# Four edits around the root-mean-square norms of a two-block transformer kernel, and a last residual sum formed by TensorE

## What is computed

```python
def rms_norm(x, g):
    y = x * lax.rsqrt(jnp.mean(x * x, axis=-1, keepdims=True) + 1e-6)
    return y * g

# first block
x = x + gt1 * mix                       # mix = concat(...) @ w_out
x = x + gt2 * swiglu(modulate(x, norm2_g, sh2, sc2), w_ffn_in, w_ffn_out)
# second block
x = x + rms_norm(merged @ w_mix_out, mix_post_g)
h = rms_norm(x, xa_pre_g)
x = x + rms_norm(mem_attention(h, ...), xa_post_g)
h = rms_norm(x, ffn_pre_g)
x = x + rms_norm(conv_ffn(h, ...), ffn_post_g)   # the output
```

## Time and profile before

| | us |
|---|---|
| runs before: lowest, median, highest of 3 | 1684.70, 1688.21, 1689.57 |
| the profiled execution | 1688.94 |
| its span | 1687.3 |

### The profile page before, as it was taken

How to read it: one execution, slowest core, us unless ns; L and a number is a source line. 1 busy time by engine, 2 the same in 40 slices (tenths; PEclk the granted TensorE clock), 3 DMA queues, 4 the chain that set the end, 5 groups by cost and what they waited for, 6 DMA issues and landing times.

```text
span 1687.3 us, 19115 instructions
## 1 busy us (share of the span) xinstructions
PE 1575.8 (93%) x7574; PEld 1243.4 (74%) x7574; DVE 944.2 (56%) x1440; ACT 725.4 (43%) x1124; POOL 139.7 (8%) x98
## 2 busy tenths in 40 slices
PE   8998989798799999999999899999887899999995
PEld 2776767587688888888878677788675688888884
DVE  3665767785744433334555555366656576257744
ACT  4453435675432222223443667455354443234421
POOL 0100212541000000000000011120011000000001
PEclk9999999699999999999999999999998899999997
DMA  9441111101524233222322222233212122332231
GB/s 370 163 162 39 50 38 63 63 1 45 192 100 147 67 111 112 98 75 88 103 100 69 63 72 67 66 122 100 75 42 71 61 90 76 113 107 93 84 103 50
DMA packets 47949, 156.59 MB, mean 93 GB/s; under 512 B 5587, under 2 KB 10323, under 8 KB 47350
## 3 DMA queue, kind: packets, MB, share of 16 engines
q1 hardware_dynamic: 47280, 152.00, 27.1%
q10 hardware_dynamic: 582, 3.38, 0.6%
HBM read 153.26 MB, written 2.10 MB: 92 GB/s over the span
## 4 chain that ended last, share of the span: by engine, by line
PE 74%; DVE 15%; ACT 7%; issue 3%; DMA 1%; POOL 0%; ACTq 0%; DVEq 0%; SPq 0%
PE pall L2079 17%; PE pall L2081 17%; PE pall L2080 17%; PE pall L2115 2%; PE pall L2562 2%; PE pall L2116 2%; PE pall L2117 1%; PE pall L2097 1%; PE pall L2098 1%; PE pall L2099 1%; PE pall L2564 1%; PE pall L2563 1%; DVE wlo L1222 1%; ACT whi L560 1%; DVE R L1235 1%
## 5 line engine op out<-in xcount | busy, mean ns | idle before, releaser
L1222 DVE TENSOR_TENSOR wlo<-raw,whi 128x1024 fp32r<-128x1024 f32 (+2 forms) x261 | 290.2, 1113 | 310.5 <-ACT whi L560 310.4
L560 ACT ACTIVATE whi<-raw 128x1024 fp32r<-128x1024 f32 (+2 forms) x263 | 246.5, 939 | 144.8 <-PE pall L2081 114.4
L2079 PE MATMUL pall<-h5h,whi 128*128 128x512 f32 x320 | 126.1, 394 | 8.4 <-DVE wlo L1222 8.4
L2080 PE MATMUL pall<-h5l,whi 128*128 128x512 f32 x320 | 125.5, 392 | 0.0
L2081 PE MATMUL pall<-h5h,wlo 128*128 128x512 f32 x320 | 125.4, 392 | 0.0
L2079 PE MATMUL pall<-h2h,whi 128*128 128x512 f32 x320 | 124.5, 389 | 0.0
L2080 PE MATMUL pall<-h2l,whi 128*128 128x512 f32 x320 | 124.5, 389 | 0.0
L2081 PE MATMUL pall<-h2h,wlo 128*128 128x512 f32 x320 | 124.5, 389 | 0.0
L2079 PEld LDWEIGHTS pall<-h5h,whi 128*128 128x128 f32 x320 | 60.7, 190 | 22.0 <-issue 9.4
L1173 ACT ACTIVATE tmp<-pall,vec 128x512 f32<-128x512 f32 x44 | 34.1, 780 | 92.8 <-DVE pall L1876 92.8
L2081 PEld LDWEIGHTS pall<-h5h,wlo 128*128 128x128 f32 x320 | 60.6, 189 | 12.8
(11 more groups left out here) (456 smaller groups left out, 3643.0 us busy)
## 6 DMA issues: line engine op xcount, KB each, us to landing
raw<-in_weights SPq DMA_DIRECT2D x204, 512.0 KB, 3.5
mraw<-in_wmod SPq DMA_DIRECT2D x32, 512.0 KB, 4.7
mod<-in_weights SPq DMA_DIRECT2D x16, 512.0 KB, 12.1
raw<-in_weights SPq DMA_DIRECT2D x25, 256.0 KB, 2.6
raw<-in_weights SPq DMA_DIRECT2D x32, 192.0 KB, 2.3
xT<-in_x SPq DMA_DIRECT2D x1, 2048.0 KB, 16.7
xT<-in_x ACTq DMA_DIRECT2D x1, 2048.0 KB, 8.2
out_y<-xT SPq DMA_DIRECT2D x8, 256.0 KB, 2.1
```

Source lines behind the costliest of these rows:

```text
L560: e.activation(whi[j % 3][:, 0:cols(j)], raw[j % 4][:, 0:cols(j)], ACT.Copy).then_inc(s.hi, 1)
L1222: e.tensor_tensor(wlo[j % 3][:, 0:n], raw[j % 4][:, 0:n], f(whi[j % 3][:, 0:n]), ALU.subtract).then_inc(s.lo_v, 1)
L2079: e.matmul(o_, a[:, kk, :], xh(k), start=(k == 0), stop=False)
L2080: e.matmul(o_, a[:, kk, :], xl(k), start=False, stop=False)
```

## The change

1. **Table and weights ahead of a root.** `use_exp()` is called after the second Silu of the modulation (ahead of the `wo` loop), and after the last activation function of each feed-forward net's second half, ahead of its down projection; `root` then finds its table in place. The `hi`/`lo` calls of `f2w` move: the first pair from beside tiles 0 and 1 to ahead of the root `xapost`, and unit 6 + 2 from the first hidden tile to ahead of the root `ffnpre`.
2. **No additions on POOL.** `add_y` is gone. DVE adds all eight tiles for g = 0 and 1.
3. **Order.** In the second post norm ACT makes the high part of a tile before its square; in the `wo` loop DVE forms residual and sum of squares before the dot product of the modulation.
4. **The last sum.** For g = 2 DVE only scales. PE multiplies `xT` tile k by the identity into bank k (float32), after the last sum of squares, and then adds the identity times the scaled tile in the same bank; ACT copies each bank to `xT`, and SP sends it.

```diff
-    "xw", "xg", "y", "yn",
+    "xw", "y", "yn", "xs", "xo",
...
-        def x_done(g, k):
-            return (s.xg, 3 * g + k // 3 + 1) if k % 3 == 0 else (s.xw, 24 + 5 * g + k - k // 3)
+        last_banks = [(at["ffnpost"] + 1 + k) % 8 for k in range(8)]
...  SP, output
-                w.wait_ge(*x_done(2, k))
+                w.wait_ge(s.xo, k + 1)
...  ACT
             table[0] = "silu"
+            use_exp()
             for m in range(8):
                 hi(J[("wo", m, 0)] + 2)
...  ACT, both feed-forward nets, between the hidden tiles and the down projection
+                if half:
+                    use_exp()
                 for m in range(8):
...  ACT
             to_y(3, "xo", 8)
+            hi(J[("f2w", 0)] + 2)
             root("xapost", bank(at["xapost"]), 512, D)
             for k in range(8):
+                w.wait_ge(s.xw, 24 + 8 + k + 1)
+                with_gain(h5h, "ffn_pre_g_2", k)
                 post_square(1, k)
-                with_gain(h5h, "ffn_pre_g_2", k)
-                if k == 0:
-                    hi(J[("f2w", 0)] + 2)
                 if k == 4:
                     hi(J[("f2w", 2)] + 2)
-            hi(J[("f2w", 4)] + 2)
+            hi(J[("f2w", 6)] + 2)
             root("ffnpre", bank(at["ffnpre"]), 512, D)
...
                     if jj == 0:
-                        hi(J[("f2w", 6)] + 2)
                         used(("f2w", 6))
...
             root("ffnpost", bank(at["ffnpost"]), 512, D)
+            for k in range(8):
+                w.wait_ge(s.xs, k + 1)
+                e.activation(xT[:, k, :], bank(last_banks[k]), ACT.Copy).then_inc(s.xo, 1)
...  DVE
                 lo(J[("wo", m, 0)] + 2)
-                dots2(("wo", m, 0))
                 used(("wo", m, 0))
                 e.scalar_tensor_tensor(xT[:, m, :], ...).then_inc(s.xw, 1)
                 add_square(0, m)
+                dots2(("wo", m, 0))
...
-                    if k % 3:
+                    if g < 2:
                         w.wait_ge(s.yn, post0[g] + k + 1)
                         e.tensor_tensor(xT[:, k, :], xT[:, k, :], y1[:, k, :], ALU.add).then_inc(s.xw, 1)
...
+            lo(J[("f2w", 0)] + 2)
             newton("xapost", bank(at["xapost"]), 512, D)
...
-                if k == 1:
-                    lo(J[("f2w", 0)] + 2)
                 if k == 5:
                     lo(J[("f2w", 2)] + 2)
...
-            lo(J[("f2w", 4)] + 2)
+            lo(J[("f2w", 6)] + 2)
             newton("ffnpre", bank(at["ffnpre"]), 512, D)
...
-                    lo(J[("f2g", jj, 0) if jj >= 2 else ("f2w", 6)] + 2)
+                    if jj >= 2:
+                        lo(J[("f2g", jj, 0)] + 2)
...  POOL
-            add_y(0, 0)
...
-            add_y(1, 8)
-            add_y(2, 24)
...  PE
             square_sums(4, "ffnpost", at["ffnpost"])
+            for k in range(8):
+                fill(last_banks[k])
+                e.matmul(bank(last_banks[k]), ident[:, :], xT[:, k, :], start=True, stop=False)
+            for k in range(8):
+                w.wait_ge(s.yn, 24 + k + 1)
+                e.matmul(bank(last_banks[k]), ident[:, :], y1[:, k, :], start=False, stop=True).then_inc(s.xs, 1)
```

More of the change, by code:

```diff
@@ L1106, in post_square @@
             def post_square(g, k):
-                w.wait_ge(*x_done(g, k))
+                w.wait_ge(s.xw, 24 + 8 * g + k + 1)
                 w.wait_ge(s.p_sq, 7 + 7 * g + k - 3)
@@ L2029, in norm_rest @@
                     e.tensor_tensor(l_[:, k, :], tmp[k % 4][:, :], f(h_[:, k, :]), ALU.subtract).then_inc(s.mlg, 1)
[L2031 to L2034, removed]
             norm_rest("mixpre", h3h, h3l)
```

## The result

The changed kernel takes 1678.49 us (median of 5, 1677.21 to 1679.19); the kernel before, run beside it, 1689.57 (median of 5, 1684.70 to 1690.59). The ratio is 0.9939, with a 95% interval of 0.9924 to 0.9955: 10.2 us less by the ratio, between 7.6 and 12.8 (the medians lie 11.1 apart). The profiled execution took 1679.19 with a span of 1677.6.

What follows compares the result with a forecast made beforehand. PE, busy 93% of the span, was taken as the bound. Terms -2.1 - 0.8 - 3.2 - 0.7 + 1.0 - 1.1 = -6.9 us took 1688.2 to 1681.3 us, range 1677.5 to 1686.5.

Steps and rivals of the forecast that it cites:

- (b): Behind the three pauses, the 0.50 clock lasts longer or shorter by up to 0.8 us each; chance 0.14, both sides.
- (c): At the end, the identity products run at the lower clock; chance 0.05.
- `wo` and its root: After `wo`: residual tile 7 earlier and table already loaded, so Ln starts at the sum of squares; -2.1 us.
- The nearer alternative, -1.3: In `wo`: DVE doesn't catch up, only the table gains, and the conversion sets Ln; -1.3 us.
- Table load of `mixpre`: Moved behind the last Silu: gains nothing since ACT idles before that Ln, and has slack there; cost 0.
- First post norm: DVE takes over POOL's three additions and loses the stretch beside them; PE's last remainder comes earlier, -0.8 us.
- Second post norm: Before `f2w`: tile 0 added at once, no remainder between tiles, no stretch beside POOL; PE starts 3.2 us earlier.
- The 0.15 of margin ahead of the root: Before root `xapost`: the moved conversion, 1.04, fits into 1.19; overrunning would delay the root by at most 1.0.
- First hidden tiles: Without the remainder after the root, DVE starts 0.73 earlier, shortening PE's 7.72 us wait after two tiles; -0.7 us.
- Last down projection: The moved table load lacks cover, so PE waits for a remainder at the second tile; +1.0 us.
- rival (d): A moved table load takes twice 1.28; the last down projection's stall becomes 2.3, total 1682.6; chance 0.04.
- The end: Identity products on PE replace the last additions; PE at 0.86 a product, not DVE, sets the end; -1.1 us.

Runs made afterwards that it cites:

- spare products: Float32 products on PE, results unread, in three long pauses: on the kernel before, ratio 0.9964; on the whole change, 0.9926; without its last table load, 0.9902 and 0.9913.
- the `wo` part alone: Kernel before with only the output projection's edits (table ahead, residual before dot product): ratio 0.9974.
- the additions alone: Kernel before with DVE making all eight additions of the second post norm, conversion of `f2w` in its old place: ratio 0.9999.
- the order alone: Kernel before with only the `f2w` conversions and remainders moved ahead of the root `xapost`, POOL still adding: ratio 0.9982.
- its repeat: The whole change measured again beside the kernel before, one semaphore name spelled otherwise and one more wait in DVE's low parts: ratio 0.9954, 1679.57 us.
- the one without the last table load: The whole change, but the last root's table is loaded in the root again, not ahead of the last down projection: ratio 0.9945.
- the best kernel: The whole change without its last table load, with 6, 9 and 8 unread float32 products in three pauses: 1670.95 us, then 1672.32.

## Why the prediction was right

1681.3 was forecast, with a range from 1677.5 to 1686.5, and 1678.49 was measured; the difference was forecast as 6.9 and came out as 10.2 and, a second time, 7.8. The sum holds by its terms, 6.5 with the clock out of the way. The total came out inside the range with luck: the first interval (7.6 to 12.8) leaves 6.9 out, most of the other 3 us came through a clock loss that the forecast doesn't have, and the range was wide enough for it. In the chances, (b) is that the lower clock (0.50) behind the three pauses lasts longer or shorter than before, by up to 0.8 us each, and (c) that the identity products at the end run at the lower clock. The 0.8 is the author's estimate, which no run shows as such; what the runs showed is a granted clock of 0.50 for 5.1, 5.1 and 5.2 us behind the three pauses of the kernel before and for 3.8, 4.2 and 5.4 in the changed one, and of 1.00 in all the identity products.

**`wo` and its root**, -2.1: -2.08, and -1.97 with spare products. DVE had caught up; its residual for tile 7 starts when PE's product is there (453.69), the chain behind it is as long as said, and Ln waits for the sum of squares alone. The nearer alternative, -1.3, would have shown Ln behind the conversion, which ends at 456.05, 0.27 ahead of it. The later transfers held nobody: the stages that follow are as long as before.

**Table load of `mixpre`**, 0: from `f1w` to the first landmark behind its root, 474.33 and 474.32.

**First post norm**, -0.8: -0.76 and -0.79.

**Second post norm**, -3.2: -3.15 twice. The total was right and the mechanism was there, but its weights were put too evenly. The prediction named three causes side by side: tile 0 is added at once, no remainder in between, no stretch. Split, the order of the conversion alone gives 2.93 and the additions 1.06. What counts is the 1.71 us that DVE stood idle for ACT's conversion behind tile 0; the remainder's own 1.2 is the smaller half. The 0.15 of margin ahead of the root held, since the conversion starts at 1267.75 and Ln at 1269.06, 0.27 after it.

**First hidden tiles**, -0.7: -1.15 in the first comparison, -0.70 with the clock out of it. The 0.45 between is the clock: the 0.50 ends 4.2 us after `f2w`'s start instead of 5.1. That the shorter pause does this isn't shown, since the `wo` part alone, with the long pause, had 3.6. So the -6.9 to which the touched stages of the first comparison sum is 6.5 and this 0.45, and the exact match with the forecast is luck.

**Last down projection**, +1.0: a wait of 0.94 where it was foretold, and 1.21 by the stage; undoing it gives 1.34 and 1.22 back. The term was 0.2 too small. The 0.94 counts from the shown end of the product ahead, pipeline tail included; from start to start it is 1.33 (1604.03 to 1605.36) instead of 0.23, which is 1.10, and the next product starts 0.31 behind instead of 0.23. That makes 1.18 of the 1.21. This part of the change is a loss. The end keeps its 15.50 without it, since PE, not the root, sets it. The load starts at 1601.60, 0.02 after the activation before it, and the conversion 0.01 behind its end, so the trace shows 1.28 for the moved load and no more than these gaps beside it; the stall of 2.3 of rival (d) didn't come.

**The end**, -1.1: -1.09. PE sets it. The granted clock stayed at 1.00 and the products 0.86 apart, so rival (c), the lower clock for the identity products, is out; DVE's scalings are done at 1669.47, 5.4 before the last write.

**The spread.** The author's estimate was a clock loss of about 2.4 for each of the three long pauses, nearly half of the 5.1 us at 0.50 behind them (the spare products took 2.4 from each of the three in the kernel before), with a shift of up to 0.8. The forecast left out the pause near 946 altogether. The 2.8 us there come and go in the same code. Up to that point three kernels are the same: the profiles of before and of the additions alone lost it (55.12 and 55.11 from 940 to 992), that of the order alone didn't (52.30), with the same idle time of PE, 2.62 to 2.64. The changed kernel, its repeat and the one without the last table load are the same there too, and the last one lost half (53.69). Window of the order alone, where before showed 0.50:

```profile
948.00:950.00 2.00, 1.80 (x8) 1.54 (x9) 0.69 (x2) 1.32 (x3) 0.00 (x0) 1.00 0.00 0
```

So whether the clock falls there differs from one execution to the next. But how often it falls does not look the same for both kernels, and this the first comparison can't show. The five kernels without spare products that have the new code at `wo` have 3 of 34 executions more than 3 us above their lowest; the three with the old code there have 35 of 81. The three profiles that had the fall are all such long executions (1688.94, 1688.44, 1681.91), and the five that hadn't are none. They also differ already ahead of that pause: from `f1w` to 940 those with the fall took 476.73, 476.75 and 476.94, those without it 476.04 to 476.46. So what the clock does behind `wo`, where the change does have a hand, goes along with what it does near 946. Part of the 3 us may well be the change's at second hand; how that comes about is open. What decides it in a single execution no run here shows; that the fall comes and goes in the same code is shown (0.50 at 948 to 950 in the profile of before, 1.00 in that of the order alone).

Of the 10.2 us of the first comparison, then, 6.5 are the stages. Nearly 4 are the clock: 2.8 near 946, 0.6 behind `wo` and 0.45 in the hidden tiles. Each of the three varies from profile to profile, and which share of them the change would bring again isn't measured; with the clock held in the three long pauses the change is worth 5.9 to 6.3.

## What to carry to other kernels

Price a change by stages from one landmark of the bound engine to the next, in a profile of each kernel, and compare the untouched stages too: what moves there isn't what you edited. It may still follow from it, as the clock's fall near 946 seems to, so count how often it happens in many executions of each kernel before you call it luck. Move a conversion ahead of a root's chain rather than behind its first tile, for an engine that waits for it there stops the whole chain (DVE stood 1.71 us here); but leave a table load where its engine would wait anyway (moved ahead of the last down projection it cost 1.2 us and gained nothing at the end). And a long pause of PE cost twice here, once as a pause and once by a granted clock of 0.50 for 3.8 to 5.4 us behind it. Filling pauses with products that nobody reads gave about as much (5 to 7 us) as all four edits. Put them into a bank that is already free: the two whose bank was not free waited 1.59 us for it here and then held up the real product by 1.4.

## What the runs showed of the hardware

- Plain float32 products held the granted clock at 1.00 in and behind the pauses that are 7.0, 11.7 and 7.7 us long in the kernel before and 5.9, 8.5 and 7.9 in the changed one, where it falls to 0.50 without them. The 26 of them in the kernel before gave it 6.1 us (4 to 8), the 23 in the change without its last table load 7.3 the first time and 5.4 the second.
- The clock also fell to 0.50 behind a pause of only 1.2 us (in the best kernel's two profiles at 935.8 and 937.7), in every profile with both the change and spare products, though not in those of the change without them, at the same place in the code.
- How much of the lower clock (0.50) is left when PE goes on varies in the same code: behind the pause ahead of `f2w`, 5.1 us in the kernel before and 3.6 in the `wo` part alone, and the stage behind it took 51.15 and 50.44.
- DVE's instructions took longer beside POOL's additions, 1.63 us against 0.69 for an addition. Taking those additions from POOL in one post norm gave 1.06 at its place. That is what tile 0, the first on the way, takes less on DVE (1.70 and 0.69), and not the end of the stretch, for which 2.0 was expected.
